# A timetable that counts TensorE's load and moves steps later, and earlier ends for the scores' pieces of blocks 2, 3, 6 and 7

## The reference, cut to what matters

```
h = rmsnorm(x);  q, k, v, xc, b_gate, c_gate = split(h @ w_in)
sb = stick_breaking(qknorm(q), qknorm(k), v)        # causal, 8 heads x 64
cv = b_gate * conv3(c_gate * xc)
x = x + concat(rmsnorm(sb), rmsnorm(cv)) @ w_out
q = (rmsnorm(x) @ w_q) -> 8 heads x (q1, q2)        # PEER
s1, s2 = q1 @ keys[0].T, q2 @ keys[1].T             # 128 scores each
v1, i1 = top_k(s1, 16); v2, i2 = top_k(s2, 16)
top_s, pos = top_k(v1[:, None] + v2[None, :], 16);  gate = softmax(top_s)
u, vv = expert_u[idx], expert_v[idx]                # 128 picks per token, 8 KB each
y = x + sum(gate * gelu(u . h2) * vv)
```

## Time and profile before

| | |
|---|---|
| median of three runs | 2874.86 us |
| the profiled execution | 2879.8 us |
| its span | 2878.0 us |
| TensorE matmul busy | 2225.2 us, 77% |
| VectorE busy | 1983.9 us, 69% |
| ScalarE busy | 1093.7 us, 38% |
| GpSimd busy | 1103.9 us, 38% |
| moved by DMA | 1183.89 MB, mean 411 GB/s |

### The profile page before, as it was taken

One profiled execution on the slowest core, in us unless ns is written; L12 is line 12 of the kernel. 1 busy time (PEld: TensorE's weight loads), 2 busy tenths in 40 slices (PEclk: granted clock), 3 DMA queues, 4 the chain that ended last, 5 costly groups with the idle time before them and its releaser, 6 DMA issues. The chain is left out here.

```text
span 2878.0 us, 29917 instructions
## 1 busy us (share of the span) xinstructions
PE 2225.2 (77%) x9210; PEld 1012.2 (35%) x9210; DVE 1983.9 (69%) x4782; ACT 1093.7 (38%) x3164; POOL 1103.9 (38%) x1037
## 2 busy tenths in 40 slices
PE   9788889778977887778986888777898656555555
PEld 6535525333532343333542244333354111111111
DVE  3757766787666668786767666888666666666654
ACT  2333432552333335562333334666233322322222
POOL 0333433343343334443344333444334444434442
PEclk9999999989998998899998999999999776777787
DMA  9999999999999999999999999999999999999998
GB/s 390 359 413 403 398 419 418 419 412 412 385 421 420 419 419 412 419 415 416 412 420 420 418 410 416 410 417 415 419 405 420 416 422 419 421 418 416 415 421 353
DMA packets 178865, 1183.89 MB, mean 411 GB/s; under 512 B 19856, under 2 KB 21520, under 8 KB 47632
## 3 DMA queue, kind: packets, MB, share of 16 engines
q0 software_dynamic: 147456, 1073.81, 90.5%
q1 hardware_dynamic: 31248, 108.17, 9.6%
HBM read 1177.70 MB, written 4.19 MB: 411 GB/s over the span
## 5 line engine op out<-in xcount | busy, mean ns | idle before, releaser
L1472 DVE CUSTOM_DVE_ANT_0 ring<-ring,h2r 128x1024 f32<-128x1024 f32 x1024 | 1249.0, 1223 | 781.2 <-DMA ring<-table_uv,idx_t 772.1
L643 POOL DMA_INDIRECT ring<-table_uv,idx_t x1024 | 1102.0, 1076 | 1755.0 <-DVE dots L1472 1128.9
L911 PE MATMUL acc<-ring,wmask 128*64 128x512 f32 x4096 | 1200.6, 715 | 578.2 <-ACT wmask L1069 574.2
L911 PEld LDWEIGHTS acc<-ring,wmask 128*64 128x64 f32 x4096 | 283.4, 153 | 1286.4 <-ACT wmask L1069 845.9
L1064 ACT ACTIVATE dots<-dots 128x2 f32<-128x2 f32 x512 | 104.1, 203 | 1530.5 <-DVE dots L1472 1528.0
L1069 ACT ACTIVATE wmask<-gmask,dots 128x64 f32<-128x64 f32 x1024 | 300.3, 340 | 48.6 <-ACT dots L1064 1.5
L1057 ACT ACTIVATE gmask<-stack,gate_t 128x64 f32<-128x64 f32 x1024 | 293.1, 334 | 0.6 <-DVE gate_t L1459 0.5
L666 PE MATMUL pt<-hT,w_held 128*128 128x256 f32 (+1 forms) x560 | 109.3, 344 | 0.0
L666 PEld LDWEIGHTS pt<-hT,w_held 128*128 128x128 f32 x560 | 88.2, 193 | 28.2 <-issue 21.1
L1064 ACT ACT_TABLE_LOAD x73 | 93.7, 1283 | 1.3
L657 PE MATMUL pz<-w_ring,hT 128*128 128x512 f32 x192 | 90.8, 615 | 0.0
(11 more groups left out here) (274 smaller groups left out, 2171.6 us busy)
## 6 DMA issues: line engine op xcount, KB each, us to landing
w_ring<-wstream SPq DMA_DIRECT2D x121, 512.0 KB
ring<-wstream SPq DMA_DIRECT2D x32, 512.0 KB, 11.7
ring<-table_uv,idx_t POOLq DMA_INDIRECT x1024
w_held<-wstream SPq DMA_DIRECT2D x11, 512.0 KB, 13.4
xs<-x_in_dram SPq DMA_DIRECT2D x8, 512.0 KB
h2r<-wstream SPq DMA_DIRECT2D x8, 512.0 KB, 14.8
scores<-wstream SPq DMA_DIRECT2D x8, 512.0 KB, 15.4
xs<-wstream SPq DMA_DIRECT2D x4, 512.0 KB, 12.3
```

What stands on the lines that cost most here:

```text
L643: nc.gpsimd.indirect_dma_start(out=ring[:, cell(t):cell(t) + 2, :].rearrange("p c d -> p (c d)"), out_offset=None, in_=table, in_offset=ba ...
L911: mm = nc.tensor.matmul(acc[HALF * i:HALF * i + HALF, half * 512:(half + 1) * 512], wmask[:, slot, :], ring[:, cell(2 * p + i) + 1, half * ...
L1472: V.tensor_tensor_reduce(u, u, h2r[:, b % H_SLOTS, i, :], 1.0, 0.0, ALU.mult, ALU.add, dots[:, t % SLOTS:t % SLOTS + 1]).then_inc(dots_don ...
```

## The change

Two things are changed in the numbers and rules that make `STEPS`. In `WHEN`, blocks 2 and 3 end the first quarter's scores at tick 212 and not 224, and the other quarters at 258 and not 262; blocks 6 and 7 end the first at 726 and not 732. And before the ranks are laid out, all front steps go through `levelled`: it walks over the ticks, adds up how long TensorE would be at work by a table of its own (`TENSOR_TIME`, and 0.97 for the mix), and holds a step back to a later tick as long as what is open is over a bound; within a front the order stays, and no front's `h` starts while the front before it has steps left. No step is added, taken away or changed inside; the ranks are laid out anew on the moved steps.

```
-WHEN = [(-1, -1, 16), (8, 66, 84), (72, 224, 262), (262, 470, 514), (521, 732, 775)]
+WHEN = [(-1, -1, 16), (8, 66, 84), (72, 212, 258), (262, 470, 514), (521, 726, 775)]
...
+TENSOR_TIME = {"w": 1.85, "v": 1.85, "scores": 1.8, "values": 1.4, "turn": 1.6, "h": 1.0, "qk_turn": 0.9, "x_turn": 1.1,
+               "key_scores": 1.4, "part": 0.3}
+TENSOR_TICK, TENSOR_SUM, TENSOR_LATE = 2.68, 0.97, 1.0
+
+
+def levelled(wanted):
+
+    out, queues, late = {}, [[] for _ in SUPER], 0.0
+    for tick in sorted(wanted):
+        for step in wanted[tick]:
+            queues[step[0]].append((tick, step))
+    for tick in range(min(wanted), BLOCKS * PICKS):
+        late = max(0.0, late + TENSOR_SUM - TENSOR_TICK) if tick >= 0 else 0.0
+        for queue in queues:
+            while queue and queue[0][0] <= tick:
+                step = queue[0][1]
+                needs = TENSOR_TIME.get(step[1], 0.0) if tick >= 0 else 0.0
+                if needs and late + needs > TENSOR_LATE + TENSOR_TIME["w"]:
+                    break
+                if step[1] == "h" and step[0] and queues[step[0] - 1]:
+                    break
+                late += needs
+                out.setdefault(tick, []).append(step)
+                queue.pop(0)
+    return out
...
+    out = levelled(out)
```

## The result

The changed kernel takes 2885.29 us (median of 7 runs, 2882.81 to 2887.86); the kernel before took 2874.86 beside it (7 runs, 2872.92 to 2878.27). The ratio is 1.0034, 95% interval 1.0023 to 1.0045: slower by some 10 us, where 10.7 won were forecast. The profiled execution took 2884.9 us, its span 2883.1.

A forecast was written before the change was run, and what follows sets the result against it. The kernel was taken as bound by bytes, so only time below 421 GB/s can be won. Terms of 6.0 + 3.5 - 1.5 - 0.5 + 2.0 + 0.5 + 0.7 = 10.7 us gave 2864.2 us, range 2854 to 2876.

The forecast's parts named there:

- first scores of blocks 2, 3: 732 to 768 us: VectorE's rank no longer waits for the scores' copy; 6.0 of 6.4 us won.
- block 1's pieces: 240 to 336 us: pieces spread to tick 89, at most one a tick; 3.5 of 6.8 us won.
- passes of blocks 2, 3: 576 to 672 us: six of eight passes now 3 ticks apart; 1.5 us more lost, bounds -2 and +15.
- blocks 4, 5: 1392 to 1404 us: clump at ticks 464 to 471 thinned, passes unmoved; 0.5 of 1.3 us won.
- pieces at 1668: 1668 to 1692 us: clump of ticks 552 to 560 thinned; 0.7 of 1.7 us won.
- blocks 6, 7: passes: 1776 to 2016 us: passes 5.5 ticks apart, were 6, a little more for VectorE; 0.5 us more lost.
- blocks 6, 7: first scores: 2112 to 2148 us: TensorE's work spread, copy 5 ticks ahead of the rank, not 3; 2.0 of 2.7 us won.
- second rival: Slower: passes of blocks 2, 3, about 560 to 650 us, need four ticks' time each; up to 15 us, chance 0.10.
- The rule weighed: Matmuls should stand back to back, so spreading pieces would be wrong; a tenth of the work at most was taken as hit.
- rival 3: TensorE's clock falls where pieces are spread, ticks 204 to 230, block 1, blocks 6, 7 in part; 2873 us, chance 0.07.
- The signs named: Profile signs: 9.50 us wait gone, rates of four stretches, GpSimd's mix wait lower, dot wait about as before, clock 0.93 or above.
- the 2 us for `h`: Tick 91: VectorE may stand still some 2 us at `h` of blocks 2, 3; costs 2 us without cover from gathers.

The follow-up runs named there:

- e1: The kernel before with only the new WHEN numbers (earlier ends for blocks 2, 3 and 6, 7), no levelling: 2880.49 us, 1.0022.
- e5: The changed kernel with four steps (two sb_sum, two conv_sum) one tick later, at odd ticks behind a mix: 2876.45 us, 1.0002.
- e7: The changed kernel with six unread matmuls keeping TensorE at work during the waits, order unchanged: 2876.06 us, 1.0004.
- e11: The changed kernel with both cures, four steps at odd ticks and six unread matmuls: 2878.77 us, 1.0005.
- e18: The changed kernel with six steps one tick later: the four of e5 and block 1's turn and conv_sum at 53: 2875.51 us, 1.0000.
- e8: The kernel before, only blocks 2, 3 drawn together from tick 148, sb_sum at odd tick 183, their steps behind it levelled: 2870.89 us, 0.9987.
- e9: e8 with blocks 6, 7 treated alike, drawn together from tick 604, sb_sum at 689: 2876.1 us, 0.9999.
- e10: e9 with the six unread matmuls of e7 added: 2877.73 us, 1.0001.
- e13: e9 with blocks 6, 7 drawn together from tick 606 and not 604, third pass's scores staying at 605: 2869.34 us, 0.9988.
- e14: e13 with ten unread matmuls on TensorE at tick 602: 2869.36 us, 0.9984.
- e3: The changed kernel with conv_sum held 5 ticks after the last conv and sb_sum 4 ticks after sb_turn: 2887.85 us, 1.0045.
- e4: The changed kernel with conv_sum alone held 5 ticks after the last conv: 2889.06 us, 1.0049.
- e6: The kernel before with sb_turn and sb_sum of blocks 2, 3 at 186 and of 6, 7 at 692, a mix behind each sum's wait: 2879.58 us, 1.0013.

## Why the prediction was wrong

What each stretch lost, length x (421 - rate) / 421 by the stretch view of each kernel's profile, as the mean over the kernels that have the same steps there (number in brackets; single ones differ by up to 4 us). "As before" and "as changed" are the timetables of that stretch.

| term of the sum | taken | stretch, us | as before | as changed | measured |
|---|---|---|---|---|---|
| first scores of blocks 2, 3 | -6.0 | 696:780 | 6.1 (6) | 0.5 (6) | -5.6 |
| block 1's pieces | -3.5 | 240:384 | 5.4 (8) | 7.3 (5) | +1.9 |
| passes of blocks 2, 3 | +1.5 | 540:672 | 3.3 (5) | 11.3 (2) | +8.0 |
| blocks 4, 5 | -0.5 | 1068:1440 | 5.5 (12) | 5.7 (2) | +0.2 |
| pieces at 1668 | -0.7 | 1440:1764 | 2.4 (10) | 2.2 (8) | -0.2 |
| blocks 6, 7: passes | +0.5 | 1764:1824 | 2.7 (6) | 6.2 (3) | +3.5 |
| | | 1824:2040 | 2.9 (5) | 5.6 (3) | +2.8 |
| blocks 6, 7: first scores | -2.0 | 2100:2160 | 2.2 (6) | 0.1 (7) | -2.1 |

The measured column adds up to +8.5 us, and the two kernels differ by 10.4 (6.6 to 12.9 by the interval).

- **First scores.** The forecast was right, mechanism and size, and e1 shows that it took both the earlier end and the thinned pieces. VectorE's wait of 9.50 us is gone: the rank's first instruction in the profile after (752.98 us, `top_v<-scores`) waited for nothing.
- **Passes of blocks 2, 3: the step that failed.** The sentence was "TensorE waits for a stick only one or two ticks after it is due instead of three, so mixes come later too"; the term was sized by level sums of work, at 1.5 us near its lower end, and measured 8.0. About half came at 624 to 672 us, where the change's `sb_sum` at 178 stands ahead of the mix of 179. The timetable as changed lost 5.5 us there and as before 1.6; with the mix put ahead or the clock held up (e5, e7, e11, e18) it was 1.4. No part of the prediction asked which step stands between a wait and the next mix, or what the clock does to it. The other half came at 552 to 624 us, where the passes stand three ticks apart: 5.8 us as changed, 6.5 with either cure or both, 1.6 as before and 1.1 with passes some five ticks apart (e8, e9, e10, e13, e14). There GpSimd waits again and again for dots, in e18 five times for 3.6 to 4.7 us (the kernel before: 3.51 and 3.34). That is the second rival's place, at some 4 us and not 15. That the passes' distance alone makes this half is not shown, since `conv_sum` stands one tick behind the last conv there as well; e3 and e4, which gave it five ticks, lost more.
- **Block 1.** "there is at most one piece a tick" was true and won nothing: 1.9 us more were lost, and the two runs with block 1 alone levelled cost 3.5 and 4.6 us. So TensorE's sum of pieces was not what made these lumps, as the term of 3.5 us had it; what did stays open.
- **Blocks 6, 7.** The first scores were right. The passes, "for VectorE, which is the busiest there", were taken at 0.5 us and measured 6.3. In 1824 to 2040 us it was again `sb_sum` at 688: with the sum at 689 2.1 us were lost in e5, 1.0 in e11 and 3.6 in e18, against 5.6. In 1764 to 1824 us order is not what cost: with `conv_sum` at 603 5.4 to 6.6 us stayed lost, and with five ticks between the last conv and the sum (e3, e4) 1.9 and 1.1 (6.5 and 8.8 over 1764 to 2040 us, against 11.8 as changed). In e5 GpSimd's 7.21 us there are a wait for VectorE's dots, so the engine named was not wrong at that place, only its price.
- **Blocks 4, 5.** The net was about nothing, as taken; a new lump of 4.7 us at 1092 was not foreseen and is given back by 1440 us.
- **The rule weighed and rival 3.** The Trainium skill's rule (page "TensorE: Matmul & The Clock Gate", section "Loop structure matters more than you think"), that a long wait between matmuls drops the clock to half, was set aside because the piece stretches stay over 90% busy. They did, at 1.00 in 732 to 768. The trace agrees with the rule at the waits: 0.50 behind 3.66 us of standing still. Where it was found, the price is not spread over pieces but paid by the mix behind a wait, so it came in the second rival's places and not in the third's. The lump at 1788 is an exception: the mix of 1796.09 us took 3.68 at a clock of 0.50, and the profile shows no wait of TensorE after the one of 2.24 us at 1776.88.
- **The signs named.** 732 to 768 at 415 or more, 2112 to 2148 above 410 and the lower total of GpSimd's waits for mixes all came true in a slower kernel; 300 to 324 is at 392. Two signs told it: the passes, 385 in 576 to 672, under the 395 given for the second rival, and GpSimd's waits for dots, 58 us more instead of about as before.
- **A sum.** The prediction's bounds add up to 20.6 us won and 15 lost (17 with the 2 us for `h`), and not to 22 and 16; the forecast doesn't hang on it.

What stays open: how far the passes' distance, and how far `conv_sum` close behind the last conv, makes the 4 us at 552 to 624; what block 1's levelling costs by; why the clock fell at 1796 us without a wait just ahead; and how much of any single profile's lump is chance of the clock. The medians of e5 and e7 are 9 us better than the change, and their profiles show 6.5 and 4.7 us of it at the four lumps.

## What to carry to other kernels

Where in-order queues are tied by semaphores, look not only at an engine's load per stretch but at each step that waits and at what stands right behind it: the work that others need goes ahead of the wait. Moving steps by one tick across such a piece of work was worth about 2 us a place here (9 us for four in e5, 4 us for two in e6). A chain over three engines also needs distance between its steps, and that half no move by one tick gave back. A total of waits, or a busy share, can improve while the kernel gets slower; count what the bound resource loses, by stretches, and take several executions before a lump of 3 us is believed. The version to keep is e8 (0.9987), the simplest of three that the intervals can't tell apart (e13 0.9988, e14 0.9984): the first scores sooner, the sum behind a mix, and nothing levelled but the pieces that had been late.

## What the runs showed of the hardware

- Waits of TensorE of 3.66 us (the change, 628 us), 4.25 (the change, 1092 us) and 6.02 (the kernel before, 1788 us) were followed by a granted clock of about 0.50, and what stood behind took up to double: a mix 3.68 us instead of 1.94, `sb_sum` 1.87 instead of 1.05. Shorter waits were followed by it in some places (2.14 us in e5 at 1788: 0.50, the sum of sixteen 3.58) and not in others (2.31 us in e14 at 1793: 1.00, the mix 1.94).
- The clock also fell to 0.50 at 1796 us of the change, where TensorE had worked since 1776.88 us without a wait that the profile shows.
- Unread matmuls of 2.86 us ahead of such a wait's end left the clock at 1.00 (e7, 618 to 632 us). The same six behind a wait of 3.63 us took 5.43 us; the sum and the mix then ran at full speed (1.86 and 1.94 us), but the stretch, 1068 to 1116 us, won nothing (6.0 us lost, 5.4 in the change).
- After the same wait of 6.02 us and the same work the clock was back 5.8 us later in one execution and not yet 8.7 us later in another.
